# A feed-forward weight ring moved by 128 bytes in its SBUF partition

## The reference, cut to what matters

```
f = (silu(x @ w_gate) * (x @ w_up)) @ w_down        # x: 512 x 1024, w_gate and w_up: 1024 x 2816, w_down: 2816 x 1024
h = h + 0.5 * rmsnorm(f, gain)
```

## The kernel before, in words

| tensor | start, bytes | modulo 256 |
|---|---|---|
| f_hidden | 56544 | 224 |
| f_ffn_before_ring, 64 bytes | 101600 | 224 |
| f_ffn_ring | 101664 | 32 |
| f_ffn_mixed, f_ffn_spare | 142624 | 32 |
| f_ffn_silu | 150816 | 32 |
| f_ffn_more | 152864 | 32 |
| f_ffn_sums (from the right side) | 172000 | 224 |
| u_low, u_high (from the right side) | 196576, 212960 | 224 |
| weight_pieces | 40160 | 224 |
| h_t_low, h_t_high (first mixer's input) | 180192, 204768 | 224 |
| mix_in_w_high, mix_in_w_low | 130208, 146592 | 160 |
| gates_w_high, gates_w_low | 130080, 134176 | 32 |
| even_qkvz_w_high, even_qkvz_w_low | 153312, 169696 | 224 |
| odd_in_w_high, odd_in_w_low | 138912, 155296 | 160 |

## Time and profile before

### The profile page before, as it was taken

One profiled execution on the slowest core, in us unless ns is written; L12 is line 12 of the kernel. 1 busy time (PEld: TensorE's weight loads), 2 busy tenths in 40 slices (PEclk: granted clock), 3 DMA queues, 4 the chain that ended last, 5 costly groups with the idle time before them and its releaser, 6 DMA issues. The chain is left out here.

```text
span 3344.3 us, 49472 instructions
## 1 busy us (share of the span) xinstructions
PE 3011.1 (90%) x20806; PEld 2436.2 (73%) x20806; DVE 1672.3 (50%) x2000; ACT 1206.0 (36%) x1836; POOL 376.9 (11%) x257
## 2 busy tenths in 40 slices
PE   5997687878776999999889999999999999799999
PEld 4985573333225998787677998799988875579997
DVE  3227652111117773435355874487533457548843
ACT  4116420000005552424344553455434444435532
POOL 2990001000000000000020000000000007200000
PEclk8998888999997999998899999999999999899999
DMA  6533159999974333131003333133322320233322
GB/s 230 180 102 153 42 213 371 427 427 426 426 323 155 101 102 116 48 101 41 1 33 108 102 103 126 53 124 102 119 71 76 91 75 2 89 100 98 106 95 76
DMA packets 215823, 479.32 MB, mean 143 GB/s; under 512 B 17809, under 2 KB 167788, under 8 KB 202558
## 3 DMA queue, kind: packets, MB, share of 16 engines
q1 hardware_dynamic: 208538, 458.43, 38.0%
q0 software_dynamic: 6768, 16.53, 1.3%
q10 hardware_dynamic: 308, 1.37, 0.1%
HBM read 457.13 MB, written 27.28 MB: 145 GB/s over the span
## 5 line engine op out<-in xcount | busy, mean ns | idle before, releaser
L453 PE MATMUL psum_banks<-u_high,f_ffn_ring 128*128 128x256 f32 (+1 forms) x1408 | 413.1, 293 | 6.7 <-DVE f_ffn_ring L3134 5.9
L454 PE MATMUL psum_banks<-u_low,f_ffn_ring 128*128 128x256 f32 (+1 forms) x1408 | 412.0, 293 | 0.0
L455 PE MATMUL psum_banks<-u_high,f_ffn_ring 128*128 128x256 f32 (+1 forms) x1408 | 411.9, 293 | 0.0
L2090 PE MATMUL psum_banks<-expert_ring,experts_x_t 128*64 128x512 f32 x1024 | 246.1, 638 | 61.5 <-DMA expert_ring<-in_expert_w_gate 34.7
L453 PEld LDWEIGHTS psum_banks<-u_high,f_ffn_ring 128*128 128x128 f32 x1408 | 267.3, 190 | 17.1 <-issue 7.1
L454 PEld LDWEIGHTS psum_banks<-u_low,f_ffn_ring 128*128 128x128 f32 x1408 | 270.0, 192 | 5.9 <-issue 0.2
L453 PE MATMUL psum_banks<-f_ffn_sums,f_ffn_ring 128*128 128x256 f32 x960 | 270.1, 281 | 1.8 <-issue 1.8
L455 PEld LDWEIGHTS psum_banks<-u_high,f_ffn_ring 128*128 128x128 f32 x1408 | 266.0, 189 | 6.0
L454 PE MATMUL psum_banks<-f_ffn_sums,f_ffn_ring 128*128 128x256 f32 x960 | 269.9, 281 | 0.0
L455 PE MATMUL psum_banks<-f_ffn_sums,f_ffn_ring 128*128 128x256 f32 x960 | 269.9, 281 | 0.0
L3150 DVE TENSOR_TENSOR f_ffn_ring<-f_ffn_more,f_ffn_ring 128x2048 fp32r<-128x2048 f32 x44 | 100.8, 2292 | 293.1 <-ACT f_ffn_ring L3044 293.1
(11 more groups left out here) (714 smaller groups left out, 7373.8 us busy)
## 6 DMA issues: line engine op xcount, KB each, us to landing
expert_ring<-in_expert_w_gate SPq DMA_DIRECT2D x32, 2048.0 KB, 36.2
expert_ring<-in_expert_w_up SPq DMA_DIRECT2D x30, 2048.0 KB, 36.6
expert_ring<-in_expert_w_down SPq DMA_DIRECT2D x28, 2048.0 KB, 35.3
f_ffn_more<-in_ffn_w_down SPq DMA_DIRECT2D x88, 512.0 KB, 4.4
weight_pieces<-in_ffn_w_gate SPq DMA_DIRECT2D x48, 512.0 KB, 4.6
weight_pieces<-in_ffn_w_up SPq DMA_DIRECT2D x48, 512.0 KB, 6.6
f_ffn_more<-in_ffn_w_gate SPq DMA_DIRECT2D x40, 512.0 KB, 5.0
f_ffn_more<-in_ffn_w_up SPq DMA_DIRECT2D x40, 512.0 KB, 6.9
```

Of the source, the lines that this page charges most:

```text
L453: nc.tensor.matmul(out, lhs.high, rhs.high, start=start, stop=False, skip_group_check=True)
L454: nc.tensor.matmul(out, lhs.high, rhs.low, start=False, stop=False, skip_group_check=True)
L455: return nc.tensor.matmul(out, lhs.low, rhs.high, start=False, stop=stop, skip_group_check=True)
L2090: last = nc.tensor.matmul(k.ps[half, bank, :], self.xt[:, q, half], self.rows_of(n, a, q * HID, HID), start=q == 0, stop=q == KD - 1)
```

## The change

Each call of `ffn_products` allocates a small tensor that nothing writes or reads, only to move what is allocated behind it. It grows from 64 to 192 bytes a partition.

```
     with Stage(nc, name) as s:
-        s.sb("before_ring", [P, 16])
+        s.sb("before_ring", [P, 48])
         ring = s.sb("ring", [P, H.RING, 2, H.COLS], F32R)
```

## The result

The changed kernel takes 3343.21 us in the median of 17 executions (3330.54 to 3349.55). The kernel before, run beside it 17 times, takes 3332.09 us (3323.72 to 3340.23). The ratio is 1.0032, interval 1.0022 to 1.0043: slower by 11 us, or 7 to 14. That is less than the 0.5% that the prediction called "no change", but the interval excludes none. The forecast was 3303.3.

The account below looks back on a forecast made before the run. The prediction took TensorE's pace alone to bound the slots. Its terms, -30.0 us (slots) and -1.6 us (classic part), sum to -31.6 us, taking 3334.9 to 3303.3 us; the range was 3296 to 3346.

Parts of the forecast that it names:

- no change: Rival: operand place only accompanies the pace, so the time stays at 3330 to 3338 us; chance 0.20.
- The slots: 6720 matmuls of 256 columns in the four feed-forwards: pace goes from 117.8 to 113.3 ns, -30.0 us.
- The base: Slots of the kernel before: 117.8 ns a matmul, measured in f0, taken to hold for the whole call.
- a restart picks it: Rival: slots have two paces, chosen at a restart, so some calls stay slow: 3311 to 3326 us; chance 0.15.
- slower: Rival: TensorE's two SBUF reads meet more often in the slots, up to 120.0 ns: 3340 to 3356 us; chance 0.15.
- The classic part: 384 matmuls of 512 columns in the feed-forwards: 233.3 to 229.2 ns each, 1.6 us gained.
- The down product: 2112 matmuls of 512 columns, both operands moved together: 0 taken, with a bound of 6.3 us lost.
- VectorE, ScalarE: Their writes to the moved ring keep their durations: 0; VectorE would be at 82% of f0's faster slots.
- DMA: f_ffn_more's loads, 4.6 us median and 8.4 at most, stay hidden behind a pair of 19.8 us: 0.
- The page's rule: TensorE has two independent SBUF read ports and never waits, so no shift alters the pace: time stays 3334.9 us.

Follow-up runs that it names:

- the third of after: The changed kernel, unaltered, profiled a third time: all four calls slow, 10 us longer than its second profile.
- the reordered kernel: Kernel before with the fourth sum's split moved behind the ring's fourth entry on ScalarE and VectorE: 3322.78 us, ratio 0.9979; with ring at 160: 3340.36 us.
- The isolated matmuls: A kernel of TensorE's matmuls alone, without the model's work, groups of 72 after pauses, stationary operand at 32 or 160: 113.3 or 117.8 ns a matmul.
- the ring alone: Against the kernel before, ring moved to 160 and the scratch tensors left at 32: 3346.75 us, ratio 1.0043.

## Why the prediction was wrong

**The slots, -30.0 us: the step that failed.** It read a pace as a property of a pair of places. Rows 6 and 7 showed 117.8 and 113.5 ns, to a tenth of a nanosecond, and "four such groups of 24" looked like four witnesses. They were not four: there is no pause between them, and in ten of the twelve profiles of whole kernels all four have one pace. (In the third of after and in the last profile of the reordered kernel the first of them ran at 117.8 and the other three at 113.3, so a change to 512 columns and back can alter the pace too.) f0's 1680 matmuls are one draw likewise, and the agreement of gates and slots to 0.1 ns was the agreement of two draws from a set of two values. The isolated matmuls put both right: distance 64 is fast in 60 of 100 groups and distance 192 in 18. The sign of the term was wrong for that reason alone. The mean over calls became some 9 us worse, not 30 better. In short, the term was a product of a count and a difference of paces where it had to be a count of calls times a difference of odds. The trace of before could have told: in the same mixer's projection, with the operands exchanged (distance 64), TensorE ran at 117.8 ns up to a short pause at 82 us and at 113.3 behind it. These two windows of 15 us lie before and behind that pause:

```profile
65.00:80.00 15.00, 15.00 (x130) 1.00 0.66 208
90.00:105.00 15.00, 15.00 (x135) 1.00 0.59 192
```

**The base, "117.8 ns as the slots are now".** All four calls at 117.8 is a bad draw of the kernel before; its two other profiles have two fast calls each. The prediction noted that the span lay 9.4 us over the median and carried the gain over unscaled. Those 9.4 us were a hint: the median execution has to be faster in something, and a call at the other pace is worth 7.5. The span lay even above the highest of the three times shown.

**The rival "a restart picks it"** held the mechanism, with a chance of 0.15. It had the fast slots of the earlier trace rows at the old places and asked whether the new ones have a second pace as well. It priced one side only: calls that stay slow after. That before has fast calls to lose didn't enter, so this rival could end no higher than 3326, and a kernel that is slower by lost draws was in no case. That 3343.2 us lies within the stated range (3296 to 3346) and within the case "slower" (3340 to 3356) is luck: that case had a different mechanism (all slots at 120.0 ns), which belongs to distance 0 and showed only when the pad was taken out.

**The classic part, -1.6 us:** as forecast, 229.0 ns in all four calls of the profile after. **The down product, 0:** as forecast, 226.9 ns. The bound of 6.3 us, had both operands not moved together, is near the 5.2 us of the ring alone. **VectorE, ScalarE, 0:** durations as before, and in f0 at 113.3 ns VectorE was busy for 155.03 of 190.40 us, 81%, against the 82% worked out; TensorE stayed the bound. **DMA, 0:** as forecast; f_ffn_more's loads land in 4.6 us in the median and 8.2 at most, against 4.6 and 8.4.

**The page's rule** that "PE and ACT never wait on anyone" (the Trainium skill, "SBUF — State Buffer", section "Who interferes with whom") was set aside on the strength of three paces, rightly. What the runs speak against is the first half of the rule as the prediction gave it, two read ports that don't depend on each other: with TensorE alone at work one form of matmul takes 113.3 to 120.0 ns by the distance of its two operands, and in the kernel distance 0 costs 0.9%.

**Left open:** what in a restart picks the pace, and whether a rise of the clock can pick it too. The length of the pause goes with it, as the 200 isolated groups show; where in the cycle the first weight load meets the stream would fit that, but no record resolves it. That it is the two reads of SBUF that meet is argued from the dependence on the difference of their addresses; no run took the weight loads away. Also why f1 and f3 before were fast in 1 call of 8 while isolated restarts at this distance are in some 6 of 10: their pause is of one kind (1.1 or 1.3 us), and a pause of one length can be nearly always fast or nearly always slow. And the difference between 7.8 and 11 us, in which the variation ahead of f0 may have a part.

## What to carry to other kernels

Where the span profiled stands apart from the timed executions, ask first what it drew: count independent restarts, not matmuls, before a pace is called a property of anything. Where TensorE is the bound and streams 256-column fp32r products against fresh 128x128 weights, compare the places of the moving and the stationary operand modulo 256 bytes: here stationary less moving 64 was best, 192 worse, 0 worst, and at 512 columns the order was another one (0 best). A pause that costs nothing by itself can cost 7 us by the pace that follows it.

## What the runs showed that was not expected

- One instruction form has two steady paces at the same places, 113.3 and 117.8 ns, each kept for up to 1680 matmuls and sometimes lost at a step only 35 ns over the pace. At the 1.2 GHz level the distances 0, 64 and 192 all took 213.3 ns a step.
- Which pace comes goes with the length of the pause ahead: at place 32, copies of 544, 576, 608 and 672 columns were followed by 113.3 ns in 31 of 31 groups, one of 624 columns in 0 of 8.
- Only the difference of the two addresses modulo 256 counts: 113.3 (most groups) at 64; 117.8 at 192; 118.3 at 32; 117.3 or 118.7 at 96; 118.6 at 128; 120.0 at 160 and at 0; 116.7 or 117.8 at 224.
- With 512 columns the distances 0, 64, 128 and 192 gave 227.0, 233.3, 232.2 and 229.0 ns (192 once 233.3), so width changes which distance is best.
- The difference from execution to execution of this kernel (3323.72 to 3340.23 us) goes, in five of six profiles of it and of the changed one, with the number of calls that drew the fast pace.
